# The hand-over between two layers of a decoder trunk, and its end: last rows, gathered pairs and their order on the engines

## What is computed

```python
def rmsnorm(x, g):
    y = x * lax.rsqrt(jnp.mean(x * x, axis=-1, keepdims=True) + EPS)
    return y * g

def moe(h, w_router, b_router, w_gate, w_up, w_down):
    ...
    expert_idx, weights = route(hf, w_router, b_router)        # two experts for each token
    ...
    def expert_block(args):
        xblk, e = args
        return (jax.nn.silu(xblk @ w_gate[e]) * (xblk @ w_up[e])) @ w_down[e]
    ...
    y_slots = yb.reshape(n_slots, d) * slot_w[:, None]
    return jax.ops.segment_sum(y_slots, slot_tok, num_segments=t)

for l in range(DEPTH):                                          # DEPTH = 2
    h = modulate(rmsnorm(x, norm1_g[l]), sh1, sc1)
    x = x + g1 * mixer(h, ...)
    h = modulate(rmsnorm(x, norm2_g[l]), sh2, sc2)
    x = x + g2 * moe(h, ...)
return rmsnorm(x, final_g)
```

## Time and profile before

| | |
|---|---|
| median of 3 runs | 1524.17 us (1522.39 to 1525.21) |
| the profiled execution | 1525.44 us |
| its span | 1523.8 us |
| TensorE busy | 1474.1 us (97%) |
| weight loads of TensorE, beside it | 1168.6 us (77%) |
| VectorE busy | 1123.7 us (74%) |
| ScalarE busy | 771.9 us (51%) |
| GpSimd busy | 115.5 us (8%) |
| mean transfer rate | 248 GB/s |

### The profile page before, as it was taken

One profiled execution on the slowest core, in us unless ns is written; L12 is line 12 of the kernel. 1 busy time (PEld: TensorE's weight loads), 2 busy tenths in 40 slices (PEclk: granted clock), 3 DMA queues, 4 the chain that ended last, 5 costly groups with the idle time before them and its releaser, 6 DMA issues.

```text
span 1523.8 us, 18999 instructions
## 1 busy us (share of the span) xinstructions
PE 1474.1 (97%) x6934; PEld 1168.6 (77%) x6934; DVE 1123.7 (74%) x1513; ACT 771.9 (51%) x1102; POOL 115.5 (8%) x139
## 2 busy tenths in 40 slices
PE   6999999999999999999889999999999999999996
PEld 1778888778878778787658888778888778777773
DVE  4584566565668999999887656754345799999997
ACT  3333433223246777777723343241233477777773
POOL 0000001000002111110000000100000111111100
PEclk9999999999999999999989999999999999999998
DMA  9566465455557999999956543542243879999995
GB/s 374 220 207 198 148 196 197 148 182 163 194 207 240 367 366 385 370 386 366 339 212 195 192 139 107 186 137 97 84 168 150 275 280 367 380 371 388 366 365 204
DMA packets 107334, 377.80 MB, mean 248 GB/s; under 512 B 16505, under 2 KB 16697, under 8 KB 106468
## 3 DMA queue, kind: packets, MB, share of 16 engines
q1 hardware_dynamic: 90720, 331.39, 60.4%
q0 software_dynamic: 15264, 40.92, 7.6%
q10 hardware_dynamic: 1252, 4.22, 0.8%
HBM read 361.62 MB, written 34.64 MB: 260 GB/s over the span
## 4 chain that ended last, share of the span: by engine, by line
PE 79%; DVE 11%; DMA 4%; ACT 3%; issue 2%; DVEq 1%; ACTq 0%; SPq 0%; POOLq 0%
PE ps L1553 23%; PE ps L1555 22%; PE ps L1554 22%; DVE w_lo L1340 5%; ACT w_hi L753 2%; PE ps L1642 2%; PE ps L1810 2%; DVE y_out L1361 1%; DMA pair<-y_rows 1%; DMA raw<-w 1%; DMA y_rows<-y_out,idx 1%; PE ps L1705 1%; PE ps L1763 1%; PE ps L1709 1%; PE ps L1784 1%
## 5 line engine op out<-in xcount | busy, mean ns | idle before, releaser
L1340 DVE TENSOR_TENSOR w_lo<-raw,w_hi 128x1024 fp32r<-128x1024 f32 x360 | 426.3, 1218 | 13.9 <-ACT w_hi L753 13.3
L753 ACT ACTIVATE w_hi<-raw 128x1024 fp32r<-128x1024 f32 x360 | 367.4, 1056 | 27.2 <-PE ps L1555 27.2
L901 DVE TENSOR_TENSOR w_lo<-raw,w_hi 128x1024 fp32r<-128x1024 f32 x136 | 166.0, 1224 | 229.2 <-ACT w_hi L582 227.7
L582 ACT ACTIVATE w_hi<-raw 128x1024 fp32r<-128x1024 f32 x136 | 142.9, 1057 | 339.4 <-PE ps L1555 337.9
L1553 PE MATMUL ps<-w_hi,hT_lo 128*128 128x512 f32 x576 | 230.0, 399 | 3.2 <-DVE hT_lo L982 3.2
L1555 PE MATMUL ps<-w_hi,hT_hi 128*128 128x512 f32 x576 | 224.8, 390 | 0.0
L1554 PE MATMUL ps<-w_lo,hT_hi 128*128 128x512 f32 x576 | 224.4, 390 | 0.0
L1553 PE MATMUL ps<-w_hi,xgT_lo 128*128 128x512 f32 x512 | 206.5, 403 | 3.7 <-DVE w_lo L901 1.0
L1555 PE MATMUL ps<-w_hi,xgT_hi 128*128 128x512 f32 x512 | 200.3, 391 | 0.0
L1554 PE MATMUL ps<-w_lo,xgT_hi 128*128 128x512 f32 x512 | 199.7, 390 | 0.0
L1553 PEld LDWEIGHTS ps<-w_hi,hT_lo 128*128 128x128 f32 x576 | 108.2, 188 | 28.9 <-DVE hT_lo L982 4.1
(11 more groups left out here) (259 smaller groups left out, 2064.7 us busy)
## 6 DMA issues: line engine op xcount, KB each, us to landing
raw<-w SPq DMA_DIRECT2D x592, 512.0 KB
h_rows<-h POOLq DMA_DIRECT2D x8, 1024.0 KB, 5.4
ahead<-w SPq DMA_DIRECT2D x4, 2048.0 KB, 10.9
x_state<-x POOLq DMA_DIRECT2D x2, 2048.0 KB, 8.2
y_rows<-x_in ACTq DMA_DIRECT2D x4, 1024.0 KB, 12.4
x<-x_state POOLq DMA_DIRECT2D x4, 1024.0 KB, 7.3
pair_early<-y_rows SPq DMA_DIRECT2D x4, 1024.0 KB, 6.4
x<-x_in SPq DMA_DIRECT2D x4, 512.0 KB, 11.5
```

The lines of the kernel that those rows point to most:

```text
L582: act.activation(w_hi[:, q % W_SLOTS], raw[:, r % RAW_SLOTS], ACT.Copy).then_inc(w_hi_ready, 1)
L753: act.activation(w_hi[:, n % W_SLOTS], expert_piece(e, n), ACT.Copy).then_inc(w_hi_ready, 1)
L901: v.tensor_tensor(w_lo[:, q % W_SLOTS], raw[:, r % RAW_SLOTS], w_hi[:, q % W_SLOTS], ALU.subtract).then_inc(raw_used, 1)
L1340: v.tensor_tensor(w_lo[:, n % W_SLOTS], expert_piece(e, n), w_hi[:, n % W_SLOTS], ALU.subtract).then_inc(raw_used, 1)
```

## The change

It does the following, in both layers unless said otherwise:

- *Last rows first.* TensorE no longer waits for `pair_2` ahead of the last rows of tiles 0 and 1; the wait and all diagonal matmuls stand behind these. On VectorE the copies of expert 15 to `y_out` stand right behind `last_hot`, where `combine` of tiles 0 and 1 stood ahead of them.
- *Combining tile by tile.* Between the layers `combine(0)` stands ahead of `last_add(0)`; `combine(1)` stands behind the norm of tile 0 and counts up `x_final` for tile 1. At the end `combine(0)` and `combine(1)` stand ahead of their tiles' adds, `combine(3)` behind the first normed output. So that the next layer can write `hT_hi` for tile 0, `pair_early` is cut in two, one in the space of `hT_hi` and one in that of `hT_lo`.
- *Expert 14's copies* stand ahead of `lo_e(4)` instead of behind it.
- *The next layer's first piece* is converted earlier: `hi(l + 1, 0)` behind the last expert's own pieces on ScalarE, `lo(l + 1, 0)` behind `last_hot` on VectorE.
- *The pair transfers* between the layers are issued behind the next layer's piece 1 instead of piece 3 (`PAIRS_AT`).

The diff, without the branch for overflowing experts on GpSimd, where only the name `pair_early` changes:

```diff
--- before.py
+++ after.py
@@ -221,7 +221,7 @@
         hid = sb("hid", [P, 512], F32, A + 24576)
         hidT_hi = sb("hidT_hi", [P, 512], F32R, A + 26624)
         hidT_lo = sb("hidT_lo", [P, 512], F32R, A + 28672)
-        pair_early = sb("pair_early", [P, 2, 2, D], F32, hT_at)
+        pair_early = [sb(f"pair_early{t}", [P, 2, D], F32, hT_at + 16384 * t) for t in range(2)]
         pair_2 = sb("pair_2", [P, 2, D], F32, A)
         pair_3 = [sb(f"pair_3{j}", [P, D], F32, A + 8192 + 8192 * j) for j in range(2)]
         hot_last = sb("hot_last", [P, NT, P], F32, A + 30720)
@@ -470,11 +470,12 @@
         STORED = (32 + 16 * (NE // 2), 32 + 16 * (NE // 2 - 1))
         PAIR_DMAS = (16, 16, 16, 32)
         ADD_BANK = (0, 4, 6, 2)
+        PAIRS_AT = 2
 
         def pair(t, j):
 
             if t < 2:
-                return pair_early[:, t, j]
+                return pair_early[t][:, j]
             return pair_2[:, j] if t == 2 else pair_3[j][:]
 
         def apart(eng):
@@ -508,7 +509,7 @@
                 for p in range(2):
                     sp.wait_ge(row_stored[p], (l + 1) * STORED[p])
                 for t in range(2):
-                    sp.dma_start(pair_early[:, t], y_tiles[t]).then_inc(pair_in[t], 16)
+                    sp.dma_start(pair_early[t][:], y_tiles[t]).then_inc(pair_in[t], 16)
                 sp.dma_start(pair_2[:], y_tiles[2]).then_inc(pair_in[2], 16)
                 for j in range(2):
                     sp.dma_start(pair_3[j][:], y_tiles[3][:, j]).then_inc(pair_in[3], 16)
@@ -524,7 +525,7 @@
                 first_load(piece)
             for l in range(DEPTH):
                 for r in range(0 if l else RAW_SLOTS, RAW_MIX + RAW_SLOTS):
-                    if l and r == W_SLOTS:
+                    if l and r == PAIRS_AT:
                         pairs_load(l - 1)
                     load(l * RAW + PRE + r, r % RAW_SLOTS, l * RAW + PRE + r + 1)
                 for i in (1, 0):
@@ -779,6 +780,8 @@
                     hi_e(13)
                     hi_e(14)
                     hi_e(15)
+                elif l < DEPTH - 1:
+                    hi(l + 1, 0, RAW_OF_W[0])
 
             def gathered_hi(E, slot):
                 for j in range(2):
@@ -865,7 +868,7 @@
                 act.nop()
                 act.activation(spare[:], k("eps"), ACT.Sqrt)
                 if l < DEPTH - 1:
-                    for q in range(W_SLOTS - 1):
+                    for q in range(1, W_SLOTS - 1):
                         hi(l + 1, q, RAW_OF_W[q])
                 act.wait_ge(hot_last_turned, l + 1)
                 act.activation(slot_last[:], ps[:, 4].rearrange("p (a b) -> p a b", a=NT), ACT.Copy).then_inc(slot_last_ready, 1)
@@ -1364,10 +1367,10 @@
                     elif before == NE - 1:
                         one.then_inc(z_half, 1)
 
-                lo_e(4)
                 if last:
                     rows_out(e - 1, 0)
                     rows_out(e - 1, 1)
+                lo_e(4)
                 lo_e(5)
                 if e and not last:
                     rows_out(e - 1, 0)
@@ -1392,8 +1395,8 @@
                     lo_e(15)
                 if last:
                     last_hot(l)
-                    for t in range(2):
-                        combine(l, t)
+                    if l < DEPTH - 1:
+                        lo(l + 1, 0, RAW_OF_W[0])
                     rows_out(e, 0)
                     rows_out(e, 1)
 
@@ -1403,16 +1406,22 @@
                     v.scalar_tensor_tensor(x[:, t], pair(t, j), weights[:, 4 * j + t:4 * j + t + 1], x[:, t], ALU.mult, ALU.add)
                     v.drain()
 
-            def combine(l, t, parts=(0, 1)):
+            def combine(l, t, complete=False):
 
                 v.wait_ge(pair_in[t], (l + 1) * PAIR_DMAS[t])
-                weighted_pair(t, w_early, parts)
-
-            def last_add(l, t):
+                weighted_pair(t, w_early)
+                if complete:
+                    v.sem_inc(x_final, 1)
+
+            def last_add(l, t, complete=True):
 
                 v.wait_ge(last_added, l * NT + (t + 1))
-                v.tensor_tensor(x[:, t].rearrange("p (h n) -> p h n", h=2), ps[:, ADD_BANK[t]:ADD_BANK[t] + 2],
-                                x[:, t].rearrange("p (h n) -> p h n", h=2), ALU.add).then_inc(x_final, 1)
+                one = v.tensor_tensor(x[:, t].rearrange("p (h n) -> p h n", h=2), ps[:, ADD_BANK[t]:ADD_BANK[t] + 2],
+                                      x[:, t].rearrange("p (h n) -> p h n", h=2), ALU.add)
+                if complete:
+                    one.then_inc(x_final, 1)
+                else:
+                    v.drain()
 
             def normed_output(t):
 
@@ -1443,13 +1452,14 @@
                     v.drain()
                     v.sem_inc(x_final, NT)
                 else:
-                    lo(l, 0, RAW_OF_W[0])
+                    combine(l - 1, 0)
                     last_add(l - 1, 0)
-                    last_add(l - 1, 1)
+                    last_add(l - 1, 1, False)
+                    lo(l, 1, RAW_OF_W[1])
                     norm_tile(l, 0, "h1", 0)
-                    lo(l, 1, RAW_OF_W[1])
+                    combine(l - 1, 1, True)
+                    norm_lo(l, "h1", 0)
                     lo(l, 2, RAW_OF_W[2])
-                    norm_lo(l, "h1", 0)
                     lo(l, 3, RAW_OF_W[3])
                     norm_tile(l, 0, "h1", 1)
                     last_add(l - 1, 2)
@@ -1492,7 +1502,7 @@
                 with v.If(count > 0):
                     overflow_tables(l)
                     v.wait_ge(w_used, l * PROD + (PROD + W_SLOTS))
-                    for t in range(2, NT):
+                    for t in range(NT):
                         v.wait_ge(pair_in[t], (l + 1) * PAIR_DMAS[t])
                     apart(v)
                     with v.Fori(0, count) as slot:
@@ -1533,12 +1543,14 @@
                 v.nop()
 
             last = DEPTH - 1
-            combine(last, 3)
+            combine(last, 0)
             last_add(last, 0)
+            combine(last, 1)
             last_add(last, 1)
             normed_output(0)
+            combine(last, 3)
+            normed_output(1)
             last_add(last, 2)
-            normed_output(1)
             last_add(last, 3)
             normed_output(2)
             normed_output(3)
@@ -1771,12 +1783,12 @@
                 for t in range(NT):
                     one = pe.transpose(ps[:, 4, t * P:(t + 1) * P], hot_last[:, t], ident)
                 one.then_inc(hot_last_turned, 1)
-                pe.wait_ge(pair_in[2], (l + 1) * PAIR_DMAS[2])
-                pair_matmuls(0)
                 pe.wait_ge(slot_last_ready, l + 1)
                 pe.wait_ge(z_half, l + 1)
                 for t in range(NT):
                     if t == 2:
+                        pe.wait_ge(pair_in[2], (l + 1) * PAIR_DMAS[2])
+                        pair_matmuls(0)
                         pair_matmuls(1)
                     for half in range(2):
                         if t == 0 and half == 1:
```

More of the change, by code:

```diff
@@ L2108, in _ @@
                         for t in range(2):
-                            pool.dma_start(pair_early[:, t], y_tiles[t]).then_inc(ov_pair, 16)
+                            pool.dma_start(pair_early[t][:], y_tiles[t]).then_inc(ov_pair, 16)
                         pool.dma_start(pair_2[:], y_tiles[2]).then_inc(ov_pair, 16)
```

## The result

The changed kernel took **1528.57 us** (median of 8 runs, 1526.9 to 1530.48) beside 1523.26 of the kernel before (8 runs, 1520.04 to 1525.21): ratio 1.004, interval 1.003 to 1.0051. It is slower by 5.3 us in the one and 3.8 in the other, where +1.1 was forecast. The two intervals just overlap; the traces are nearer to the second.

What follows compares the result with a forecast made beforehand. TensorE, busy 97% of the span, was taken as the bound, its largest wait being for gathered rows. Between the layers +2.8 and at the end -1.7 gave +1.1: 1525.2 us for the median, range 1521.8 to 1528.8.

Steps and rivals of the forecast that it cites:

- rival D: Between the layers: piece 2 does not hold ScalarE, `slot_last` ready at 758.9; sum -9.0, 1515.1 us; chance 0.08.
- step 3: ScalarE between the layers: `slot_last` waits for piece 2, landing 13.8 us after the scatter; TensorE starts last rows at 766.9.
- step 2: Between the layers: expert 14's scatter takes 6.5 us and lands at 751.4, ends 749.4 and 754.05.
- Earlier scatter: VectorE between the layers: expert 14's copies and scatter come one piece, 1.13 us, earlier; 0.15 us of the price remains.
- Rival A: Between the layers: scatter stays at 9.11 us, landing at 754.05; sum +3.7, 1527.9 us; chance 0.13.
- C: Between the layers: scatter takes 4.5 us, landing at 749.4; sum -0.9, 1523.3 us; chance 0.1.
- TensorE from s: Between the layers: restart at half clock, 24 records take 13.07 us, the first 8 release the adds after 6.4.
- s: Moment between the layers when TensorE starts its last rows, forecast at 766.9 against a restart at 765.21 before.
- VectorE behind that: Between the layers: tile 1's combine now follows tile 0's norm; tile 1's transposes 20.7 us after TensorE's restart, +2.8 us.
- Rival B: TensorE's clock falls again in a 2.0 us gap before tile 1's transposes; sum +2.2, 1526.4 us; chance 0.2.
- The end: Behind the last layer: last rows start at full clock, VectorE ends last, last norm at 1517.74 against 1519.48: -1.7 us.

Runs made afterwards that it cites:

- the first trace of before: Profiled execution of the unchanged kernel before, on which the prediction rested: 1525.44 us.
- the three traces with the changed hand-over: Changed kernel unedited, twice (1528.57 and 1527.72 us), and changed kernel with the old end, only the work between the layers changed (1531.64 us).
- the three with the old hand-over: Kernel before unedited, two traces (1525.44 and 1522.79 us), and kernel before with only the end changed (1521.95 us); work between the layers as before.
- the second comparison: Changed kernel, unedited, measured again with the experiments: 1527.72 us (10 runs) beside 1523.96 of the kernel before (28 runs), ratio 1.0022.
- the filler: Changed kernel plus nine matmuls without use between the turned `hot_last` and the wait for `slot_last`: 1524.8 us beside the changed kernel's 1527.72.

## Why the prediction was wrong

The mechanism was right: the new wait was named, with its place and its order, and rival D fell (`slot_last` was not ready at 758.5). The sizes were off, all to one side: the landing of piece 2 (step 3) above all, and the execution that it was counted from (step 7). With step 3 alone mended the sum is +2.4, with step 2 as well +2.7; only with step 7 does it pass the bound of 3.05 that parts "slower" from "same". The time itself lies inside the range, near its upper end.

1. *Earlier scatter.* Issued at 745.93, 12.77 us ahead of the transposes of `hot_last`, against 11.42 in the first trace of before: 1.35 sooner, where 1.13 and the slip of 0.15 were forecast. Right, though the times don't show its worth.
2. *Landing of the scatter.* 6.78, 6.89 and 6.67 us in the three traces with the changed hand-over; 6.5 was taken. **0.3 too little.** Rivals A (9.11) and C (4.5) fell both. The estimate of 4.6 us from the Trainium skill's page DMA: Bandwidth & Descriptors was never reached: in none of the traces does the scatter of this place take less than 6.17.
3. *Landing of piece 2, and with it the restart.* This is the step that failed. The sum "bytes ahead of it, at 411 GB/s" gave 13.8 us behind the scatter's landing; it was 15.35, 15.04 and 15.0 in the three. **1.3 too little.** The part of it that was measured in the trace of before, 10.0 us to `pair_2`, held (10.0, 9.8 and 9.8), and piece 2 landed 1.3 us behind the last pair transfer, as summed. What was too short is the part for the two transfers of `pair_3`. From issue to landing they took, in the changed kernel (issued at 754.17 and 754.80, landed at 764.5 and 766.8) and before (756.64 and 757.3, landed at 766.4 and 767.7):

```profile
DMA to landing us min/median/max: 10.3/11.1/12.0
```

```profile
DMA to landing us min/median/max: 9.8/10.1/10.4
```

   They were in 4.0, 4.0 and 3.8 us behind `pair_2` in the three traces, where 2.55 were summed and before took 2.5. The windows show 396 to 414 GB/s in that time of the first trace: 1.6 MB, where the two are 1.05 MB. All that was queued besides were the pieces behind them. I read this as these pieces taking a share before what is ahead of them is complete, and no run here isolates it. The kernel before with the pairs moved speaks against it as the whole cause: six loads had been issued behind its pairs as well, and there the two took 2.6 us and piece 2 landed at 14.3. Why they were late stays open.
4. *TensorE from s.* 13.12 us to the norm's transposes, 13.07 forecast; the second add at s + 6.46, 6.4 forecast. Right.
5. *VectorE behind that.* s + 20.73, 20.41 and 21.00; 20.7 forecast. Right, and so is the combination of tile 1, "just done when `hT_hi` is there": putting it back into the wait gained nothing. Rival B fell: the gap was 1.95 us long, and the clock stayed full.
6. *The end.* 1.7 us, 1.7 forecast, and VectorE is its bound, with one pause of 0.45 us for ScalarE ahead of the norm of tile 2, as said. That the number fits is in part luck: the last norm was forecast 19.4 to 19.5 us behind `hot_last` (1498.3 to 1517.74) and comes at 19.16, and it was counted from an end of 21.36 where the mean is 20.87.
7. *What it was compared with.* The steps were subtracted from one execution, in which the scatter had taken 9.11 us. Measured as the distance from one `hot_last` to the other, that execution is 740.63, the mean of the three with the old hand-over 739.54, of the three with the new one 744.99. So +5.45 is what the hand-over costs, where the forecast has +2.8: 1.1 for the unusual base, 1.6 for steps 2 and 3. With the end, +5.45 - 1.7 = **+3.75**, which is the 3.8 of the second comparison; the first gave 5.3, and 1.5 of that have no cause that the traces show. (Rival A's +3.7 meets the second comparison by chance: the scatter of 9.11 us on which it rests did not come.) The prediction saw the 9.11 as "the longest of all 30", used it against rival A, and yet left it in the time from which it counted.

Where the 10.4 us of the new wait come from and what they cost can now be told from the other side. With all four pieces ahead of the pairs the time is 1518.7; three ahead 1521.0; two ahead 1527.7 to 1528.6, of which 2.9 are the clock. So the change holds a gain of 4.7 us against the kernel before (hand-over and end together), and the number that says where the pairs are loaded turns it into a loss.

## What to carry to other kernels

When a transfer is moved ahead of another, look up who waits for the one that now stands behind, on an engine that works in order, and list what stands behind *that* wait; taking the held instruction out is not enough, since the next one in the queue is held in its place (`slot_last` first, then the row deviations). A landing summed from the bytes ahead of it can be too early: summed at 13.8 us, it came at 14.3 to 15.4 in all ten traces that have a weight piece right behind the pairs. And before steps are subtracted from one trace, its unusual values are to be set to the usual ones on both sides of the subtraction.

## What the hardware showed beyond that

- *How long the clock stays down after a restart varies, for the same order of work.* From the restart to the full clock: 5.5, 4.9 and 6.0 us in the three traces with the changed hand-over, 3.3 and 2.9 in those with the combination or the scatter put back. It moves tile 1's transposes from 19.42 us behind the restart (2.9) to 21.00 (6.0) and is as large as what single steps of this change are worth. The Trainium skill's page TensorE: Matmul & The Clock Gate, HAM oscillation, tells of a stretch behind a wait for a DMA that starts cold each time; the trace agrees (the first 8 records at 6.42 us instead of 3.70), also where the wait is ScalarE's and only by way of it the DMA's.
- *Busy work that came early in a wait did not warm what came after it.* The pair matmuls at 761.69 left 4.12 us idle, and the restart was cold; the filler left 1.66 us, and it was not.
- *Loads behind the scatter cost it little.* With the earlier issue it took 6.17 us with four pieces ahead of the pairs, 7.39 with three, and 6.54 to 7.96 with two (seven traces); with the later issue 7.63 to 9.11 with four and 7.20 and 7.26 with two. The spread for one kernel is as large as any effect of their number.
